# Attention scores of a float32 transformer block pair in two products instead of three or four: queries and keys laid out anew

## The reference, cut to what matters

```python
# first attention: 8 windowed heads (2 key heads shared by 4 query heads each), 8 causal ("moba") heads
s = einsum('bnqhgd,bnkhd->bnhgqk', qb, kk) * 64 ** -0.5          # windowed, + bias, mask, sink in the softmax
s_past, s_own = q_c . k_sel * 64 ** -0.5, q_c . k_own * 64 ** -0.5   # causal, + bias, softmax over both

# second attention ("forgetting"): F = cumsum over tokens of log_sigmoid(h @ w_f + b_f), one row for each head
q = (h @ w_q).reshape(...) * 64 ** -0.5
logits = einsum("bhqd,bhkd->bhqk", q, k) + F[:, :, q0:kend, None] - F[:, :, None, :kend]
logits = where(kpos <= qpos, logits, -inf);  p = softmax(logits);  o = p @ v
```

## Time and profile before

| what | value |
|---|---|
| median of 3 runs | 2061.42 us (2061.41 to 2062.13) |
| the profiled execution, its own time | 2059.95 us |
| its span, first to last instruction | 2058.2 us |
| PE busy | 1951.2 us (95%) |
| PEld, weight loads (beside PE) | 1604.3 us (78%) |
| DVE busy | 1175.2 us (57%) |
| ACT busy | 755.2 us (37%) |
| POOL busy | 336.8 us (16%) |
| mean granted PE clock | 0.977 |
| first attention, its heads | about 76 to 242 us |
| second attention, its heads | about 1424 to 1608 us |

### The profile page before, as it was taken

One profiled execution on the slowest core, in us unless ns is written; L12 is line 12 of the kernel. 1 busy time (PEld: TensorE's weight loads), 2 busy tenths in 40 slices (PEclk: granted clock), 3 DMA queues, 4 the chain that ended last, 5 costly groups with the idle time before them and its releaser, 6 DMA issues.

```text
span 2058.2 us, 22473 instructions
## 1 busy us (share of the span) xinstructions
PE 1951.2 (95%) x9056; PEld 1604.3 (78%) x9056; DVE 1175.2 (57%) x1865; ACT 755.2 (37%) x1141; POOL 336.8 (16%) x297
## 2 busy tenths in 40 slices
PE   4999999899999999998999999999998889999996
PEld 3888888688888877886788888768887668888885
DVE  7566555576667645666655644565666554333445
ACT  4566522342222234223322222364555342222223
POOL 4423111011111102004000000237222130000002
PEclk9999999999999999999999999989999989999997
DMA  9422365265655424421654433232111222322321
GB/s 330 131 80 67 133 235 201 82 248 202 225 187 221 143 82 184 150 100 57 245 184 174 173 103 99 86 103 87 42 42 42 82 66 98 103 86 98 102 82 41
DMA packets 126120, 267.55 MB, mean 130 GB/s; under 512 B 4463, under 2 KB 33151, under 8 KB 126016
## 3 DMA queue, kind: packets, MB, share of 16 engines
q1 hardware_dynamic: 121056, 248.59, 35.1%
q0 software_dynamic: 4960, 17.53, 2.4%
HBM read 261.84 MB, written 8.45 MB: 131 GB/s over the span
## 4 chain that ended last, share of the span: by engine, by line
PE 80%; DVE 10%; ACT 8%; issue 1%; DMA 1%; POOL 0%; SPq 0%; ACTq 0%; DVEq 0%; POOLq 0%
PE ps L599 25%; PE ps L600 25%; PE ps L601 25%; DVE t L1572 2%; ACT t L1161 2%; DVE t L1606 1%; ACT t L1074 1%; DVE t L1546 1%; DVE t L1563 1%; ACT t L1115 1%; PE ps L714 1%; ACT t L1193 1%; DVE t L1560 1%; DVE t L1611 1%; PE ps L677 1%
## 5 line engine op out<-in xcount | busy, mean ns | idle before, releaser
L599 PE MATMUL ps<-t 128*128 128x512 f32 (+1 forms) x2584 | 1004.5, 389 | 32.0 <-DVE t L1546 16.2
L601 PE MATMUL ps<-t 128*128 128x512 f32 (+1 forms) x2584 | 996.5, 386 | 0.0
L600 PE MATMUL ps<-t 128*128 128x512 f32 (+1 forms) x2584 | 996.3, 386 | 0.0
L599 PEld LDWEIGHTS ps<-t 128*128 128x128 f32 x2584 | 488.3, 189 | 138.1 <-issue 22.8
L601 PEld LDWEIGHTS ps<-t 128*128 128x128 f32 x2584 | 487.9, 189 | 103.0
L600 PEld LDWEIGHTS ps<-t 128*128 128x128 f32 x2584 | 488.1, 189 | 97.6 <-issue 1.0
L1449 DVE TENSOR_TENSOR t<-t 128x2048 fp32r<-128x2048 f32 x133 | 305.0, 2293 | 447.1 <-ACT t L1067 446.9
L1067 ACT ACTIVATE t<-t 128x2048 fp32r<-128x2048 f32 x133 | 254.3, 1912 | 617.7 <-PE ps L601 613.8
L1509 DVE SCALAR_TENSOR_TENSOR t<-ps,t 128x512 f32<-128x512 f32 x184 | 132.6, 748 | 97.8 <-PE ps L601 89.2
L1461 DVE CUSTOM_DVE_ANT_0 t<-t 128x1024 f32<-128x1024 f32 x144 | 175.2, 1258 | 10.6 <-DMA t<-in_ada 4.5
L1572 DVE TENSOR_TENSOR t<-ps,t 64x512 fp32r<-64x512 f32 (+4 forms) x183 | 103.9, 578 | 103.4 <-ACT t L1193 48.6
(11 more groups left out here) (160 smaller groups left out, 1436.3 us busy)
## 6 DMA issues: line engine op xcount, KB each, us to landing
t<-in_ada SPq DMA_DIRECT2D x48, 1024.0 KB, 6.0
t<-in_gate SPq DMA_DIRECT2D x22, 1024.0 KB, 5.1
t<-in_up SPq DMA_DIRECT2D x22, 1024.0 KB, 5.2
t<-in_down SPq DMA_DIRECT2D x22, 1024.0 KB, 5.0
t<-in_w_in SPq DMA_DIRECT2D x17, 1024.0 KB, 5.9
t<-in_w_mlp_in SPq DMA_DIRECT2D x16, 1024.0 KB, 5.4
t<-in_w_mlp_out SPq DMA_DIRECT2D x16, 1024.0 KB, 5.1
t<-in_ada_t POOLq DMA_DIRECT2D x13, 1024.0 KB, 6.3
```

The lines of the kernel that those rows point to most:

```text
L599: pe.matmul(o, wh, xh, start=first, stop=False)
L600: pe.matmul(o, wh, xl, start=False, stop=False)
L601: return pe.matmul(o, wl, xh, start=False, stop=last)
```

## The change

The low half of a head's queries now lies in the 64 rows that the other head had: `Qa`, `Qb` and `Q2` have one tile for each head, high half in the head's own 64 rows, low half in the other 64. The high half of a head's keys lies twice, in both halves of the rows, and the low half once; the other 64 rows beside the low half hold zeros in the first attention (4 instead of 8 memsets for two key buffers) and rows of the gates in the second. So one product gives high by high plus low by high, and a second one gives high by low, in the second attention with the gates in it: `QF`, made by POOL for each head, has the head's high queries in its own rows and the head's rows of `AF` in the others.

```diff
-            Qa = sb(outer, [2, 4, T], R)
-            Qb = sb(outer, [2, 4, T], R)
+            Qa = sb(outer, [8, T], R)
+            Qb = sb(outer, [8, T], R)
...
-                AFr = [sb(inner, [T], R) for _ in range(2)]
-                BF = sb(inner, [T], R)
+                QF = [sb(inner, [T], R) for _ in range(2)]
...
                 o = psum[bank][:, 0:N]
-                pe.matmul(o, hd["q"][0][:, tok], hd["k"][0][:, kr], start=True, stop=False)
-                pe.matmul(o, hd["q"][1][:, tok], hd["k"][0][:, kr], start=False, stop=False)
-                ins = pe.matmul(o, hd["q"][0][:, tok], hd["k"][1][:, kr], start=False, stop=st == 1)
+                pe.matmul(o, hd["q"][:, tok], hd["k"][0][:, kr], start=True, stop=False)
+                q = hd["q"]
                 if st == 2:
+                    q = QF[h % 2]
                     on.wait_ge(p_fox, "af", h)
-                    on.wait_ge(a_gate, "bf")
-                    ins = pe.matmul(o, AFr[h % 2][:, tok], BF[:, kr], start=False, stop=True)
+                    if hd["zero"]:
+                        on.wait_ge(p_fox, "bf", 1)
+                    else:
+                        on.wait_ge(a_gate, "bf", 0)
...
+                pe.matmul(o, q[:, tok], hd["k"][1][:, kr], start=False, stop=True).then_inc(mm.sem, mm.up("score", st, h, i))
...
+        own = [slice(0, 64), slice(64, 128)]
         def halves_of_keys(name, bank, i):
             kv = k_view(KV1[0] if name == "ka" else kv_of[name])
             for odd in range(2):
-                r, n = slice(64 * odd, 64 * odd + 64), 2 * i + odd
-                yield n, psum[bank][r, :], kv[r, 0, n, :], kv[r, 1, n, :]
+                n = 2 * i + odd
+                his = [kv[own[p], 0, n, :] for p in (odd, 1 - odd)]
+                if name == "ka":
+                    los = [(kv[own[p], 1, 2 * n + p, :], kv[own[p], 0, n, :]) for p in range(2)]
+                else:
+                    los = [(kv[own[odd], 1, n, :], his[0])]
+                yield n, psum[bank][own[odd], :], his, los
+
+        def halves_of_queries(name, t):
+            q = {"qa": Qa, "qb": Qb, "q2": Q2}[name]
+            for odd in range(2):
+                yield own[odd], q[own[odd], 2 * t + odd, :], q[own[1 - odd], 2 * t + odd, :]
...
             def queries(name, t, bank, *event):
-                act.activation(of_queries(name)[:, 0, t, :], psum[bank][:, :], ACT.Copy, scale=QSCALE).then_inc(
-                    a_hi.sem, a_hi.up(name, t))
+                for rows, hi, lo in halves_of_queries(name, t):
+                    ins = act.activation(hi, psum[bank][rows, :], ACT.Copy, scale=QSCALE)
+                ins.then_inc(a_hi.sem, a_hi.up(name, t))
             def keys(name, bank, n, i):
-                for k, src, hi, lo in halves_of_keys(name, bank, i):
-                    act.activation(hi, src, ACT.Copy).then_inc(a_hi.sem, a_hi.up(name, k))
+                for k, src, his, los in halves_of_keys(name, bank, i):
+                    for hi in his:
+                        ins = act.activation(hi, src, ACT.Copy)
+                    ins.then_inc(a_hi.sem, a_hi.up(name, k))
...
             on.wait_ge(d_fox, "sums")
-            act.activation(fhi[0:16, :], fr, ACT.Copy).then_inc(a_gate.sem, a_gate.up("fhi"))
-            act.activation(fF, fhi[0:16, :].bitcast(F), ACT.Copy).then_inc(a_gate.sem, a_gate.up("fF"))
-            act.activation(AF[0:16, :], fF, ACT.Copy)
-            act.activation(AF[32:48, :], z3, ACT.Copy)
-            act.activation(BF[64:80, :], fF, ACT.Copy, scale=-1.0)
-            act.activation(BF[96:112, :], z3, ACT.Copy, scale=-1.0).then_inc(a_gate.sem, a_gate.up("bf"))
+            act.activation(fhi[0:32, :], fr, ACT.Copy).then_inc(a_gate.sem, a_gate.up("fhi"))
+            on.wait_ge(d_fox, "sum rows")
+            for r, one, gates in gate_places(KV2[0]):
+                ins = act.activation(gates, twice(AF[0:32, :]), ACT.Copy, scale=-1.0)
+            ins.then_inc(a_gate.sem, a_gate.up("bf", 0))
...
-            for v in zero_places(KV2[0]):
-                ins = dve.memset(v, 0.0)
...
-            dve.tensor_tensor(z3, fr, fhi[0:16, :].bitcast(F), ALU.subtract).then_inc(d_fox.sem, d_fox.up("lo"))
+            dve.tensor_tensor(z3, fr, fhi[0:32, :].bitcast(F), ALU.subtract).then_inc(d_fox.sem, d_fox.up("lo"))
+            dve.tensor_scalar(z3, z3, lower, 1.0, ALU.mult, ALU.mult).then_inc(d_fox.sem, d_fox.up("lower rows"))
+            for r in (0, 64):
+                dve.scalar_tensor_tensor(out=AF[r:r + 32, :], in0=fhi[0:32, :].bitcast(F), scalar=upper, in1=z3, op0=ALU.mult,
+                                         op1=ALU.add).then_inc(d_fox.sem, d_fox.up("sum rows", r))
...
-                pool.tensor_scalar(AFr[h % 2][:, :], AF, hmask[:, h:h + 1], 1.0, ALU.mult, ALU.mult).then_inc(
+                pool.tensor_copy(QF[h % 2][mine, :], Q2[mine, h, :]).then_inc(p_fox.sem, p_fox.up("queries", h))
+                pool.tensor_scalar(QF[h % 2][other, :], AF[other, :], hmask[other, h:h + 1], 1.0, ALU.mult, ALU.mult).then_inc(
                     p_fox.sem, p_fox.up("af", h))
```

More of the change, by code:

```diff
@@ L36 @@
 NV = _n
[L37 to L38 removed]
+C_ID, C_ONE, C_MASK, C_HEAD, C_LOW = 0, 128, 256, 768, 784
+NC = 786
 SKEW = P * 648
@@ L504, in head2 @@
             t, kv, c = 2 * g + n // 2, KV2[g % 2], blocks[n // 2]
-            return dict(kind="causal", sink=None, q=(Q2[:, 0, t, :], Q2[:, 1, t, :]), qt=("q2", t),
+            return dict(kind="causal", sink=None, q=Q2[:, h, :], qt=("q2", t),
+                        out=(Q2[:, 2 * t, :], Q2[:, 2 * t + 1, :]),
                         k=(k_view(kv)[:, 0, n, :], k_view(kv)[:, 1, n, :]), kt=(f"fk{g}", n), zero=g % 2,
                         v=lambda j: (v_view(kv)[:, 0, j, c], v_view(kv)[:, 1, j, c]),
-                        vt=[(f"fv{g}", p) for p in range(2)], r0=64 * (n % 2))
+                        vt=[(f"fv{g}", p) for p in range(2)], r0=64 * (n % 2), s0=64 * (n % 2))
         heads = {1: [head1(h) for h in range(16)], 2: [head2(h) for h in range(16)]}
@@ L1012, in zero_places, with gate_places, twice @@
         def zero_places(kv):
-            for s in range(2):
-                for odd in range(2):
-                    r = slice(0, 64) if odd else slice(64, 128)
-                    yield k_view(kv)[r, s, odd::2, :].bitcast(F)
+            for odd in range(2):
+                yield k_view(kv)[own[1 - odd], 1, odd::2, :].bitcast(F)
+        def gate_places(kv):
+            for odd in range(2):
+                r = 64 * (1 - odd)
+                yield r, k_view(kv)[r:r + 32, 1, odd::2, :], k_view(kv)[r + 32:r + 64, 1, odd::2, :]
+        def twice(rows):
+            return rows.rearrange("p (a n) -> p a n", a=1).broadcast_to([32, 2, T])
         def weights_turned(st, h, g, bank):
@@ L2166, in program_pool @@
             on.wait_ge(p_fox, "one")
[L2167 to L2170 removed]
+            for r, one, gates in gate_places(KV2[0]):
+                ins = pool.memset(one.bitcast(F), 1.0)
             ins.then_inc(p_fox.sem, p_fox.up("ones of BF"))
```

152 lines of the change are left out of this document (75 added, 77 removed).

## The result

The changed kernel takes 2069.58 us (median of 7 runs, 2065.16 to 2071.77) against 2061.41 us of the kernel before on the same chip (2058.74 to 2064.14). The ratio is 1.0038, with a 95% interval from 1.0027 to 1.0050: 8 us slower, where 2072 was forecast. The profiled execution took 2068.54 us, its span is 2066.7.

The account below looks back on a forecast made before the run. PE holds 80% of the chain of waits, but inside attention heads ACT and DVE alternating set the time. Gains of 7.7 us against costs of 19.3, less about 1 overlap, gave +10.6: 2072 us, own range 2067 to 2077, 8-in-10 range 2056 to 2081.

Parts of the forecast that it names:

- fewer products, all: Both attentions: removing 192 products, 29.4 us of PE's time, shortens the kernel by only 7.7 us.
- the start of the first attention: Eight score tiles where PE is ahead of DVE on the path, each 0.12 us shorter: -0.9 us.
- the head behind that start: First attention's next head, still partly set by PE: -0.4 us, between 0 and -0.5.
- the start of the second: Second attention's start: seven tiles after the first, with two products less each: -2.3 us.
- heads of 11.04: Two second-attention heads beside the projection of values, down to the first attention's 10.65 us: -0.4 each.
- heads of 13.24: Two second-attention heads that evacuate keys: ACT's 1.07 us wait for PE goes, -1.0 each.
- ten key evacuations: Inside the heads: two more ACT copies in each evacuation, on the ACT-DVE chain, 1.1 us each: +11.0 us.
- queries, all: Split query evacuations: +2.4 us for heads 8 to 15, +1.0 before the first attention, +0.6 in the second.
- gates and clock: At the gates: +2.3 us for added instructions and keys, +2.0 for a lower PE clock after 3.4 us idle.
- overlap: About 1 us less cost, as two additions in the same heads meet slack that the faster PE opens.
- The rival that PE's rate decides: Everywhere: the whole 29.4 us are gained, less exposed costs outside the heads; about 2036 us, chance 5%.
- The rival of the clock: Above all last heads and gates: PE idles more, low clock returns, 6 to 8 us more, 2079; chance 15%.

Follow-up runs that it names:

- before, fewer products: The kernel before with only the change's fewer score products, nothing else copied or moved: 2053.79 us, ratio 0.9963.
- keys once: The changed kernel without the second copy of the high keys in the ten evacuations inside the attentions, low queries' product left out there: 2058.71 us.
- before, keys copied twice: The kernel before with ACT copying each high key of k1, k0, fk1 to fk3 again into unread spare rows: 2069.67 us, ratio 1.0039.
- before, queries split: The kernel before with each queries' evacuation made in two 64-row instructions on ACT and on DVE: 2067.64 us, ratio 1.0029.
- moving the conversion: The changed kernel with ACT's conversion of the weight slot moved ahead of its wait for the gates' rows: 2063.36 us, ratio 1.0012.
- all improvements: The changed kernel with POOL making the second key copies and the conversion earlier: 2052.20, again 2055.15 us; with more evacuation copies on POOL too: 2051.90 us.

## Why the prediction was right, and where it was wrong

The sign, the range and the place of the costs were right. That 2072 lies 2.4 us from the median is partly luck: the sum had +10.6 where the change costs 17 to 20 us at equal addresses, so it was 6 to 10 too small, and a gain that it did not have, 9 to 12 us, came in. Without that gain the time would have lain outside the forecast's own range of 2067 to 2077 (2083.31, at the old addresses). By term:

| term | forecast | measured, and by which kernel |
|---|---|---|
| fewer products, all | -7.7 | -7.6, between 5.2 and 10.1; its parts in the profile add up to 6 (before, fewer products) |
| of these the start of the first attention | -0.9 | 0.0 (first score product to first reciprocal 9.00, now 8.97) |
| the head behind that start | -0.4 | -0.35 |
| the start of the second | -2.3 | -2.35 (12.35 to 10.00) |
| the head behind it | -1.3 | -0.7 |
| heads of 11.04, each | -0.4 | -0.4 |
| heads of 13.24, each | -1.0 | -0.85 |
| ten key evacuations | +11.0 | +11.5 (keys once); +8.0 with the old products (before, keys copied twice) |
| queries, all | +4.0 | +6.0 (before, queries split) |
| gates and clock | +4.3 | +5.35 (changed against before, fewer products); moving the conversion gives back 6.9 |
| overlap | -1 | not measured by itself |
| clock behind the last heads | 0, a rival of +6 to 8 | +2.0 |
| start address of operands | not in the sum | -9 to -12 |

**What bounded the stages.** The comparison of the earlier trace rows across the two attentions held: with three or two products the two kinds of head take 11.2 and 10.65 us, with four 11.2 and 11.04. The rival that PE's rate decides is refuted by the kernel with fewer products alone, and so is the rule of the Trainium skill that I had weighed (Perfetto Trace Analysis, "Identifying the Most-Contended Engine"): weight loads were busy 87 to 88% there, and taking 29 us of PE's work away gave 7.6.

**The rival of the clock.** The low level did come more often: the mean granted clock is 0.972 after 0.977, and 0.83 over 1610 to 1700 us, behind the last heads, where the kernel before has 0.89 over 1600 to 1690. But the last heads did not get longer (9.63 and 9.35 us after 9.64 and 9.36), so the rival's 6 to 8 us are not there. From the last reciprocal to the end it is 456.5 us, against 454.4 in the kernel before at the same addresses: 2 us that my sum had put at nothing.

**The keys.** The largest term was right in size and mechanism; 45.8% of the 5.2 us of chain above is those copies.

**The start of the first attention.** The scores did come earlier: in the kernel before with fewer products DVE's wait for them fell from 2.0 us to 1.1, and its last maximum is done 0.9 us sooner behind the first score product. But the first reciprocal came no earlier, and the time is in the one instruction between them, DVE's addition of the sinks to the four sums (L1618), which now starts together with a weight piece of POOL. DVE and POOL in the kernel before:

```profile
84.63 0.36 DVE L1618 TENSOR_TENSOR t<-t 128x4 f32<-128x4 f32 x1
...
83.65 1.31 POOL L1972 TENSOR_TENSOR t<-t 128x512 fp32r<-128x512 f32 x1
```

And in that kernel with fewer products:

```profile
84.24 1.28 DVE L1618 TENSOR_TENSOR t<-t 128x4 f32<-128x4 f32 x1
...
84.20 1.29 POOL L1972 TENSOR_TENSOR t<-t 128x512 fp32r<-128x512 f32 x1
```

Both times DVE is done 0.03 us after POOL (84.99 after 84.96, 85.52 after 85.49); where no POOL instruction runs beside it, this addition takes 0.15 us (88.50 in the kernel before). I had counted a wait as a gain without asking what comes second there, and what came second was POOL.

**The queries.** The step that failed is the price by place. I took 0.3, 0.5, 1.1 and 0.5 us for the four evacuations, arguing that where ACT's weight pieces follow only ACT's copy counts. With the queries split in the kernel before, the periods of the first four heads rose by 1.06, 1.01, 1.38 and 0.72 us (3.66, 10.92, 9.78, 9.73 to 4.72, 11.93, 11.16, 10.45), 4.1 and not 2.4 in all: at least a full ACT instruction (0.6) each time, and in three of the four most or all of DVE's (0.67) too. Outside, two of PE's waits that I had priced grew as follows, in the changed kernel against the earlier trace rows:

```profile
65.12 0.50 PE L611 MATMUL ps<-t 128*128 128x512 f32 x1 [2.10 <-DVE t L1475]
...
1380.32 0.42 PE L611 MATMUL ps<-t 128*32 128x512 f32 x1 [1.86 <-DVE t L1603]
```

2.10 after 0.74 us (forecast +1.0) and 1.86 after 0.80 (forecast +0.6), so +1.4 and +1.1. A copy of 64 rows takes 0.6 us and not 0.5, which explains 0.2 of the first; the rest is not traced to an instruction.

**The gates.** I had placed the delay ahead of the first score product, with PE idle 3.4 us. The first product came as soon as before; PE's wait came after the scores, at the low half of the values, and was 4.93 us. Counted from the gates' own product, PE went on 3.6 us later than before, not 2.3. Of that, 2.8 are in front of DVE's conversion and 0.8 in it, as it took 3.11 us and not 2.29: POOL's gate rows (L2079) run beside it, instructions of the change that my sum of the gates did not have. The first of them (1429.16 to 1430.20) starts just ahead of the conversion, and the second, 1.99 us and not 1.04, ends only 0.9 behind it. The low clock came as foreseen, 0.50 in 1434 to 1437 us, and what is left of the 5.35 beside the delay, 1.7, is about the +2.0 that I had put down for it; no run measures it by itself.

**What was missed.** The diff has the two columns in it, in a line that I read as a table and not as an allocation. The trace before had the hint, products 233 ns apart in some stretches and 227 in others at the same clock, and I looked at busy time and the clock alone.

## What to carry to other kernels

Before pricing work that leaves an engine, compare two stages of the same kernel that differ in just that work: it gave 7.7 us for the products, inside the measured 5.2 to 10.1, where busy shares pointed to 29. Where two engines pass work to and fro, an instruction added on either can cost its full length however idle both look (0.4 to 0.6 us for each key copy of 0.6 here), and an idle third engine is the place for it. But if that is POOL, look at what DVE does beside it: here the conversion, the scalings and even the addition of four sums waited. An edit that changes the size of one allocation moves all that follow, so a comparison of two kernels needs one more, with the old program and the new addresses: here two unused columns in the old kernel (2050.1 us, ratio 0.9943) did as much as the new layout with all improvements (2051.9 to 2055.2, 0.9949 to 0.9967), and both beat the two kernels compared above.

## What the hardware showed that I had not expected

- Products of 128x512 whose moving operand starts 32 bytes past a multiple of 64 start 233.3 ns apart (kernel before; 233.0 in the changed kernel moved there); at a multiple of 64 it is 228.9 (changed kernel, and the one before with two columns more), at full granted clock in all. The Trainium skill (SBUF — State Buffer, "Operand start alignment") says of start addresses what is legal, that of speed nothing was timed; this is a case in which the speed differs, by 2%.
- DVE's conversion 128x2048 took 3.11 us beside POOL's products of 32x1024 and 2.29 without them; an addition of 128x4 took 1.28 us when it started with POOL's subtraction of 128x512 and 0.15 alone; three scalings took 3.78 us beside three such subtractions and 1.83 with less of them. The Trainium skill (SBUF — State Buffer, "SBUF: two separate sides") states that DVE and GpSimd share a port pair as an exclusive lock, also for a DVE instruction with two inputs in SBUF while GpSimd reads there, and that the later one is blocked for the whole of the other. The conversion and the addition, which have two inputs, agree: the addition ended 0.03 us after POOL's subtraction, and POOL's second product took 1.99 us beside the conversion and 1.04 when it came first. The scalings have one input, so this clause does not cover them, and that they are slower beside POOL rests on the trace alone.
- Around 4.93 us of idle PE (1428.27 to 1433.20 us) the granted clock was 0.52 over 1430.5 to 1437.3 us, so it fell while PE stood idle; around 1.09 us in the kernel before it did not fall.
